# State-space stage of a two-block transformer kernel: place of the gate projections, of the squares' sum and of the last output unit

## The reference, cut to what matters

```
def mamba2_mixer(h, w_in, conv_w, conv_b, dt_bias, A_log, D_skip, g_out, w_out):
    proj = h @ w_in                                     # 1024 -> 5152
    z, xBC, dt_raw = jnp.split(proj, [D_INNER, D_INNER + CONV_DIM], axis=-1)
    xBC = jax.nn.silu(causal_depthwise_conv(xBC, conv_w, conv_b))
    xs, Bm, Cm = jnp.split(xBC, ...)                    # 2048, 4 x 128, 4 x 128
    ...
    y = ssd_chunked_scan(xh, dt, A, Bm, Cm)             # 32 heads of 64
    y = y + D_skip[:, None] * xh
    y = y.reshape(Bsz, S, D_INNER) * jax.nn.silu(z)
    y = y.reshape(Bsz, S, SSM_GROUPS, D_INNER // SSM_GROUPS)
    y = y * lax.rsqrt(jnp.mean(y * y, axis=-1, keepdims=True) + EPS)
    y = y.reshape(Bsz, S, D_INNER) * g_out
    return y @ w_out                                    # 2048 -> 1024
```

## Time and profile before

| | |
|---|---|
| median of 3 runs | 2084.71 us |
| profiled execution | 2081.91 us, its span 2080.1 us |
| TensorE busy | 1903.5 us, 92% of the span |
| VectorE busy | 991.9 us, 48% |
| ScalarE busy | 793.4 us, 38% |
| GpSimd busy | 700.2 us, 34% |
| mean granted TensorE clock | 0.957 |
| the state-space stage with its first projections | about 0 to 560 us |

### The profile page before, as it was taken

One profiled execution on the slowest core, in us unless ns is written; L12 is line 12 of the kernel. 1 busy time (PEld: TensorE's weight loads), 2 busy tenths in 40 slices (PEclk: granted clock), 3 DMA queues, 4 the chain that ended last, 5 costly groups with the idle time before them and its releaser, 6 DMA issues.

```text
span 2080.1 us, 25547 instructions
## 1 busy us (share of the span) xinstructions
PE 1903.5 (92%) x9155; PEld 1490.3 (72%) x9155; DVE 991.9 (48%) x1635; ACT 793.4 (38%) x1416; POOL 700.2 (34%) x795
## 2 busy tenths in 40 slices
PE   6998999988699998999999899898888989999998
PEld 3776767766467655777878777687776767888887
DVE  5567475364561675346658625555571133121222
ACT  4334233343454555335552133434342334232231
POOL 0642433332235200531104322222202454565553
PEclk8999999999899999999999999999989999999999
DMA  5232332211122100211018621111112332333332
GB/s 165 81 109 66 92 100 61 61 51 51 33 61 81 56 21 11 73 51 31 21 31 265 201 53 39 51 31 31 31 31 61 91 91 72 95 97 94 97 97 95
DMA packets 238796, 152.53 MB, mean 73 GB/s; under 512 B 7997, under 2 KB 223046, under 8 KB 238694
## 3 DMA queue, kind: packets, MB, share of 16 engines
q1 hardware_dynamic: 225894, 126.00, 21.2%
q10 hardware_dynamic: 12800, 25.17, 3.6%
HBM read 149.05 MB, written 2.10 MB: 73 GB/s over the span
## 4 chain that ended last, share of the span: by engine, by line
PE 66%; issue 13%; DVE 8%; POOL 7%; ACT 5%; DMA 0%; SPq 0%; DVEq 0%; POOLq 0%; ACTq 0%
PE ps L576 16%; PE ps L577 16%; PE ps L578 16%; POOL wl L539 7%; PE ps L2314 2%; PE ps L1414 2%; PE ps L1884 2%; PE ps L1383 1%; PE ps L1866 1%; PE ps L1873 1%; DVE al L685 1%; PE ps L604 1%; PE ps L1403 1%; ACT wh L552 1%; DVE norm_v L680 1%
## 5 line engine op out<-in xcount | busy, mean ns | idle before, releaser
L539 POOL TENSOR_TENSOR wl<-raw,wh 128x256 fp32r<-128x256 f32 (+1 forms) x775 | 676.7, 903 | 1315.4 <-ACT wh L552 1315.4
L576 PE MATMUL ps<-ah,wh 128*128 128x512 f32 (+1 forms) x1208 | 499.4, 413 | 50.6 <-DVE al L685 14.2
L577 PE MATMUL ps<-al,wh 128*128 128x512 f32 (+1 forms) x1208 | 482.2, 399 | 0.0
L578 PE MATMUL ps<-ah,wl 128*128 128x512 f32 (+1 forms) x1208 | 481.9, 399 | 0.0
L552 ACT ACTIVATE wh<-raw 128x1024 fp32r<-128x1024 f32 (+1 forms) x220 | 230.9, 1049 | 373.1 <-PE ps L578 360.8
L576 PEld LDWEIGHTS ps<-ah,wh 128*128 128x128 f32 (+1 forms) x1208 | 232.9, 193 | 129.2 <-issue 44.0
L578 PEld LDWEIGHTS ps<-ah,wl 128*128 128x128 f32 (+1 forms) x1208 | 232.3, 192 | 53.4 <-issue 0.8
L577 PEld LDWEIGHTS ps<-al,wh 128*128 128x128 f32 (+1 forms) x1208 | 233.6, 193 | 47.4 <-issue 1.4
L576 PE MATMUL ps<-bh,wh 128*128 128x512 f32 (+1 forms) x588 | 238.9, 406 | 22.9 <-DVE resid L1260 7.1
L577 PE MATMUL ps<-bl,wh 128*128 128x512 f32 (+1 forms) x588 | 234.1, 398 | 0.0
L578 PE MATMUL ps<-bh,wl 128*128 128x512 f32 (+1 forms) x588 | 233.5, 397 | 0.0
(11 more groups left out here) (368 smaller groups left out, 2749.9 us busy)
## 6 DMA issues: line engine op xcount, KB each, us to landing
raw<-w_mlp SPq DMA_DIRECT2D x64, 512.0 KB, 4.0
raw<-w_in SPq DMA_DIRECT2D x52, 512.0 KB, 3.8
raw<-ssm_w_in SPq DMA_DIRECT2D x40, 512.0 KB, 3.8
ada_late<-w_ada ACTq DMA_DIRECT2D x16, 1024.0 KB, 6.1
ada_raw<-w_ada ACTq DMA_DIRECT2D x16, 512.0 KB, 3.6
raw<-ssm_w_out SPq DMA_DIRECT2D x16, 512.0 KB, 3.3
raw<-mla_w_in SPq DMA_DIRECT2D x11, 512.0 KB, 3.9
raw<-mla_w_out SPq DMA_DIRECT2D x8, 512.0 KB, 3.6
```

The lines of the kernel that those rows point to most:

```text
L539: ins_ = nc.gpsimd.tensor_tensor(wl[:, s, part], raw[:, s, part], wh[:, s, part].bitcast(F32), ALU.subtract)
L576: nc.tensor.matmul(dst, w_hi[k], x_hi[k], start=k == 0, stop=False)
L577: nc.tensor.matmul(dst, w_hi[k], x_lo[k], start=False, stop=False)
L578: ins = nc.tensor.matmul(dst, w_lo[k], x_hi[k], start=False, stop=k == n - 1)
```

## The change

Five things move, and one small thing is tidied:
- The first gate projection (unit 6) goes from behind the heads to between `exponents`' end and `outputs` of the last head, `outputs(g, 7)`. Unit 7 takes the place behind the heads, and `squares`, the modulation, units 8 and 9 follow.
- ScalarE writes the 4 squares to 4 buffers (2 of `norm_sq`, 2 of `norm_v`), all ahead of `split_ahead(6)`. VectorE adds them up by three additions (two behind its heads, the third behind `heads_in`), and TensorE sums the result over the channels by one matmul.
- `turn_x` uses banks 6, 7, 5, 6 for its 4 blocks, where it used 6, 7, 6, 7.
- Output unit 11 of group 2 goes between `turn_x(3)` and `turn_b(3)`, unit 12 to head 0 of group 3, and unit 13 behind all heads of group 3, with the sum of squares between its two halves. Its two additions to `resid` stand inside VectorE's last `normed`.
- The last group's normed tiles go to chunks 4 to 7 of `bh` and `bl`; ScalarE's `split_ahead` for unit 13 stands behind the last `high`.
- The zeroing of `wgk` counts on another semaphore.

Its core as a diff:

```diff
+        XT_BANKS = (6, 7, 5, 6)
...
+        normed_at = lambda g: 4 if g == GROUPS - 1 else 0
...
-                    if t >= 2:
-                        pe.wait_ge(sem("xt_used"), g * TT + t - 1)
+                    if t == 2 and g:
+                        pe.wait_ge(sem("mod_taken"), min(g, CTX_BLOCKS // 2))
+                    elif t == 3:
+                        pe.wait_ge(sem("xt_used"), g * TT + 1)
                     for c in range(4):
-                        ins_ = nc.tensor.transpose(bank(6 + t % 2)[:, c * P:(c + 1) * P], xs[:, c, t * P:(t + 1) * P], ident[:])
+                        ins_ = nc.tensor.transpose(bank(XT_BANKS[t])[:, c * P:(c + 1) * P], xs[:, c, t * P:(t + 1) * P], ident[:])
                     ins_.then_inc(sem("xt_ready"), 1)
...
-            def squares(g, p):
-                pe.wait_ge(sem("gsq_ready"), g * 4 + p + 1)
-                nc.tensor.matmul(bank(4), ones[:], norm_sq[:, p % 2], start=p == 0, stop=p == 3).then_inc(sem("gsq_used"), 1)
-
-            def output(stage, i, g, n0, uses, w):
+            def squares(g):
+                pe.wait_ge(sem("gsq_summed"), g * 3 + 3)
+                nc.tensor.matmul(bank(4), ones[:], norm_sq[:, 0], start=True, stop=True).then_inc(sem("gsq_used"), 1)
+
+            def output(stage, i, g, n0, uses, w, between=None):
...
-                    ins_ = project(bank(c), stage, n0 + w, chunk(bh), chunk(bl), 4, 2 * P, slice(c * P, (c + 1) * P),
+                    ins_ = project(bank(c), stage, n0 + w, chunk(bh, normed_at(g)), chunk(bl, normed_at(g)), 4, 2 * P, slice(c * P, (c + 1) * P),
                                    before=chunk_ready if w == c == 0 else None)
+                    if between is not None and c == 0:
+                        between()
                 ins_.then_inc(unit_done, 1)
...
                     if g < GROUPS - 1 and h < 6:
                         projection("ssm", g, h)
-                    elif g == GROUPS - 1 and h < 3:
-                        output("ssm", GROUPS - 2, GROUPS - 2, 10, 5, h + 1)
+                    elif g == GROUPS - 1 and h == 0:
+                        output("ssm", GROUPS - 2, GROUPS - 2, 10, 5, 2)
                     if h + 2 < GH:
                         exponents(g, h + 2)
+                    elif g < GROUPS - 1 and h == GH - 1:
+                        projection("ssm", g, 6)
                     outputs(g, h)
-                for p in range(3):
-                    squares(g, p)
...
                 heads(g)
-                projection("ssm", g, 6)
-                squares(g, 3)
+                projection("ssm", g, 7)
+                squares(g)
                 if g < CTX_BLOCKS // 2:
                     modulation(2 * g)
                     modulation(2 * g + 1)
-                for n in range(7, 10):
+                for n in range(8, 10):
                     projection("ssm", g, n)
                 output("ssm", g, g, 10, 5, 0)
                 if g < GROUPS - 2:
                     output("ssm", g, g, 10, 5, 1)
                 turn_x(g + 1)
-                if g < GROUPS - 2:
-                    output("ssm", g, g, 10, 5, 2)
+                output("ssm", g, g, 10, 5, 2 if g < GROUPS - 2 else 1)
                 turn_b(g + 1)
                 if g < GROUPS - 2:
                     output("ssm", g, g, 10, 5, 3)
             heads(GROUPS - 1)
-            squares(GROUPS - 1, 3)
+            output("ssm", GROUPS - 2, GROUPS - 2, 10, 5, 3, lambda: squares(GROUPS - 1))
...
-                    elif g == GROUPS - 1 and 1 <= h <= 3:
-                        split_ahead(act, "ssm", GROUPS - 2, 10 + h)
+                    elif g == GROUPS - 1 and h == 1:
+                        split_ahead(act, "ssm", GROUPS - 2, 12)
...
             def square(g, p):
                 act.wait_ge(sem("gated"), g * 4 + p + 1)
-                act.wait_ge(sem("gsq_used"), g * 4 + max(p - 1, 0) + AHEAD)
-                nc.scalar.activation(norm_sq[:, p % 2], xs[:, p], ACT.Square).then_inc(sem("gsq_ready"), 1)
+                if g and p == 2:
+                    act.wait_ge(sem("glo_ready"), g * 4)
+                nc.scalar.activation((norm_sq[:, p] if p < 2 else norm_v[:, p - 2]), xs[:, p], ACT.Square).then_inc(sem("gsq_ready"), 1)
 
             def scale(g):
 
-                act.wait_ge(sem("gsq_used"), g * 4 + 4 + AHEAD)
+                act.wait_ge(sem("gsq_used"), g + 1 + AHEAD)
...
                 heads(g)
-                for p in range(3):
+                for p in range(4):
                     square(g, p)
                 split_ahead(act, "ssm", g, 6)
-                square(g, 3)
                 scale(g)
...
-                for w in range(1 if g == GROUPS - 2 else 4):
+                for w in range(2 if g == GROUPS - 2 else 4):
                     split_ahead(act, "ssm", g, 10 + w)
...
                 high(GROUPS - 1, p)
+            split_ahead(act, "ssm", GROUPS - 2, 13)
...
-                    elif g == GROUPS - 1 and 1 <= h <= 3:
-                        output("ssm", GROUPS - 2, 10, h)
+                    elif g == GROUPS - 1 and h == 1:
+                        output("ssm", GROUPS - 2, 10, 2)
...
+            def sum_squares(g, parts):
+
+                for p in parts:
+                    dve.wait_ge(sem("gsq_ready"), g * 4 + p + 1)
+                    if p > 1:
+                        dve.wait_ge(sem("gsq_summed"), g * 3 + p - 1)
+                    nc.vector.tensor_tensor(norm_sq[:, 0], norm_sq[:, 0], norm_sq[:, 1] if p == 1 else norm_v[:, p - 2],
+                                            ALU.add).then_inc(sem("gsq_summed"), 1)
+
+            def normed(g, between=None):
 
                 dve.wait_ge(sem("grstd"), g * 2 + 2)
                 for p in range(5):
+                    if between is not None and 1 <= p <= 2:
+                        between(p - 1)
...
                 heads(g)
+                sum_squares(g, (1, 2))
                 heads_in(g + 1)
+                sum_squares(g, (3,))
                 convolve("ssm", g, g + 1, 4)
...
-                if g < GROUPS - 2:
-                    output("ssm", g, 10, 2)
+                output("ssm", g, 10, 2 if g < GROUPS - 2 else 1)
                 take_b(g + 1)
...
             heads(GROUPS - 1)
-            normed(GROUPS - 1)
+            sum_squares(GROUPS - 1, (1, 2, 3))
+
+            def last_of_group(c):
+
+                if c:
+                    dve.wait_ge(unit_done, unit("ssm", GROUPS - 2, 13) + 1 + CREDIT)
+                nc.vector.tensor_tensor(resid[:, 6 + c], resid[:, 6 + c], bank(c), ALU.add).then_inc(acc_free[c], 1)
+
+            normed(GROUPS - 1, last_of_group)
```

17 lines of the change are left out of this document (8 added, 9 removed).

## The result

The changed kernel takes 2048.37 us (median of 4, 2042.71 to 2050.88). The kernel before took 2083.85 us on the same chip (median of 4, 2080.11 to 2087.13). The ratio is 0.9827, with an interval of 0.9809 to 0.9844: about 36 us faster, where 27.1 were forecast. The profiled execution took 2042.7 us with a span of 2040.8, against 2081.9 and 2080.1.

The account below looks back on a forecast made before the run. TensorE, busy for 92% of the 2080.1 us span, was taken as the bound. Groups 0 and 1 (12.8), group 2 (2.9), `turn_x` (2.9) and group 3 (8.5) sum to 27.1 us: 2084.7 to 2057.6 us, range 2050 to 2067.

Parts of the forecast that it names:

- What bounds the kernel: TensorE, busy for 92% of the span; a microsecond taken from it in the state-space stage is one off the end.
- The hole of the last head: Groups 0 and 1: unit 6 fills the 5.1 us wait for VectorE's product; last head runs at full clock in 1.9 us.
- Squares on VectorE: Groups 0 and 1: three additions, 2.25 us, hidden behind unit 7; 2.9 us of sums and a 1.7 us wait go.
- Unit 8: Groups 0 and 1: starts at 187.1, where unit 7 started at 192.8; half clock costing 2.2 us kept, ends at 194.8.
- Unit 9: Groups 0 and 1: starts 8.4 us earlier, behind a new 3.0 us wait for GpSimd; gain 6.4 us each.
- The clock term: Half clock behind the new wait ahead of unit 9: 2.0 us per group, between nothing and 2.85 us.
- The rival without half clock: Unit 9's new waits of about 3 us cost no clock: gain 33, 2051.6 us; chance 0.14.
- Group 2: Unit 9 starts 2.0 us earlier, unit 8 idles 4.5 us for gate 0; gain 2.9 us, bounds 0 and 5.
- `turn_x`: Third block's own bank starts the fourth 1.2 us earlier in `turn_x(1)` and `(2)`, 0.5 in `(0)`; 2.9 us, bounds 1.5 and 3.5.
- Group 3: Heads end 10.4 us earlier, first last unit 8.8; 8.5 us after the delayed low parts, bounds 6.5 and 9.5.
- VectorE the bound: GpSimd slows VectorE's convolutions: groups 0 and 1 give 3.2 us each, group 2 nothing; 17.8 us, 2066.9 us; chance 0.18.
- Repeated half clock: Clock stays at 0.50 through units 8, 9 and output units ahead of `turn_x`: 47 us more, 2104.8 us; chance 0.03.

Follow-up runs that it names:

- the filled kernel: The kernel before, same order, with useless matmuls put ahead of seven kinds of wait and no wait removed: 2069.31 us, ratio 0.9927.
- the kernel with the table: The changed kernel with unit 9's rounding right behind gate 0 and one load of a ScalarE table holding Ln and Exp: 2043.64 us, ratio 0.9819.
- the best one: The changed kernel with unit 9's early rounding, single Ln/Exp table load, and in group 2 B's convolution at head 5 and 14 useless matmuls ahead of unit 8: 2039.61 us.

## Why the prediction fell short

The sum of the terms was 27.1 us; against the first trace of the kernel before, the stage of the changed kernel gives 35.3 in its first trace, 32.0 in its second and 33.8 in its third. The measured 2048.4 us lie 1.6 below the low end of the range, 2050. By term, in us gained:

| stretch | forecast | first trace | second trace | third trace |
|---|---|---|---|---|
| `turn_x` to head 6, groups 0, 1, 2 | 0.5, 1.2, 1.2 | 0.3, 2.6, 2.8 | 0.3, 2.6, 2.8 | 0.3, 2.6, 2.8 |
| head 6 to next `turn_x`, groups 0, 1 | 6.4, 6.4 | 8.7, 7.7 | 5.8, 9.3 | 7.1, 7.7 |
| the same, group 2 | 2.9 | 4.9 | 3.3 | 4.9 |
| group 3 up to the first last unit | 8.8 | 9.3 | 9.3 | 9.3 |
| the last units | -0.3 | -0.9 | -1.5 | -0.9 |

- **What bounds the kernel.** Right. The end moved with TensorE's waits and clock in this stage. The rest of the program moved by 3 us (1521.4 to 1518.1), as it does between runs.
- **The hole of the last head.** Right: last head at 173.0 behind unit 6, no wait, full clock; TensorE's waits for this product fall from 13.7 us to 1.2.
- **Squares on VectorE.** Right: hidden behind unit 7. Wrong in two details. I had GpSimd idle beside them, but it starts unit 8's split at 178.28, ahead of the third addition, which still took 0.68 us. And the two convolutions beside that split took 7.2 us (179.11 to 186.27) where they took 5.7 before; I had allowed 0.5. So the norm came 0.7 us later from head 6 than forecast. The split took 4.70 us, but unit 8 waits for the gate anyway.
- **Unit 8.** It starts 18.75 us behind head 6, forecast 18.7, released by gate 0. The modulation, 3.63 us at full clock where I had left 4.78, no longer sets its start. The unit took 8.6 us in group 0 of the first trace and 7.3 in the other two, against 7.7. Neither counts, since the wait behind it takes up the difference.
- **Unit 9.** Counted from head 6 it starts 8.3 us earlier (8.4 forecast), partly by luck: the norm was 0.7 us late, the step from the norm to the rounding took 5.1 us and not 6.1, that from the rounding to the start 5.5 and not 5.1. The wait is 2.2 to 3.5 us. The clock term, 2.0 us a group, was mis-sized: 0, 1.6, 0 in the first trace, 2.9, 0, 1.6 in the second, 1.6, 1.6, 0 in the third. Against my 6.0 us for the three groups that is 4.4, 1.5 and 2.8 us less. The rival without half clock held for two of three in the first trace, and its 2051.6 us were closer than mine.
- **Group 2.** Start of unit 9 2.1 us earlier (2.0 forecast), gate wait 4.63 (4.5). What was off is the clock: unit 9 went from 8.50 us to 5.74, 7.33 and 5.76, a gain of 2.8 or 1.2 where I took 0.85. This is the group 2 part of the term just named.
- **`turn_x`.** The step that failed in every trace: I priced it by its wait alone, 1.2 us each in groups 1 and 2. The output unit behind it ran 1.1 to 1.6 us long in the kernel before, by granted clock 0.78, in all three of its traces, and that went too. The term is 5.7 us against 2.9. It could have been seen: I read the clock only behind waits of over 2 us and behind one of 1.7 us that happened to be free, and took that for all of 1.7 us. The banks alone are not what makes this half clock, though: with them undone in the changed kernel these two stretches are 1.2 us longer each (71.1 against 70.0), as I priced them, and the units still take 5.7 us.
- **Group 3.** Right in its sum (heads 10.7 us earlier, forecast 10.4; sum to first unit 5.4, forecast 5.6).
- **VectorE the bound.** Wrong for this kernel by its size: groups 0 and 1 gained 5.8 to 9.3 us where this rival had 3.2. But right in its cause, since the convolutions were slowed by 1.4 us beside GpSimd, and right one step on: with unit 9's wait removed, the waits come back for VectorE in groups 0 and 1.
- **Repeated half clock.** Refuted: no unit of the stage took longer than 8.6 us, and behind units 8 and 9 the next one took 5.6 us every time. The Trainium skill, TensorE: Matmul & The Clock Gate, section HAM oscillation, tells of a kernel in which every new gap throttled it anew. The trace does not agree for the gaps here: four of nine waits ahead of unit 9 were not paid at all.

The error is one-sided: 27.1 against 32.0 to 35.3 us. Of the 8.2, 4.9 and 6.7 us missing in the three traces, `turn_x` holds 2.8 each time and the clock of unit 9 holds 4.4, 1.5 and 2.8. So both steps that failed are prices of the clock behind a wait, one set to nothing and one too high, and the mechanism of waits was right. That idle time costs clock at the last heads of groups 1 and 2 and ahead of unit 9 of group 2 is shown by the filled kernel; how the gain of the changed kernel splits is read from rows. What decides whether the clock falls behind a wait of 1.7 us stays open.

## What to carry to other kernels

When TensorE is the bound and waits, price each wait with the unit behind it: compare that unit's length with the same unit elsewhere, also behind short waits, and count the difference as the most that removing the wait can give on top. Where it doesn't come out the same in a second trace of the same kernel, put it in the range, not in the sum. And before you remove a wait, look at which engine is next late: here 7 us of waits for GpSimd were removed and came back one or two units later, as waits for GpSimd, VectorE and ScalarE.

## What the runs showed of the hardware

- Useless matmuls in idle time made the kernel 15 us faster (0.9927) and a stage 13 us shorter, of which some 8 us are left for the filling itself.
- Behind the one-column fp32 matmuls of the modulation (x32, 3.63 us at full clock) and 1.17 us of idle the unit took 7.3 and 8.6 us in traces of the changed kernel. With no wait between, it took 7.3 us or 5.7: in the kernel with the table, 5.70 in group 0 and 7.32 in group 1, in the best one 7.32 and 5.69.
- A fall of the clock behind a wait of 1.7 us repeats: three traces of one kernel agree within 0.1 us, while kernels with the same wait differ by up to 1.6 us. Behind a wait of 2.72 us in group 3 the unit took 7.3 us in three kernels and 5.7 in two. What decides it stays open.
- A unit's loss by clock can be free: unit 8 took 7.3 to 8.6 us in groups 0 and 1, and with the wait behind it 10.8 us in all six cases.
- GpSimd and VectorE slow each other: 2.77 us become 4.70 for four pieces of a split, 0.75 become 1.2 for an operation of VectorE, 5.7 become 7.2 for two of its convolutions.
